# Cached sequences' values: fp32r products with both parts of the probabilities in one stationary, in two blocks of four page pairs

## What is computed

```python
ckv = concat([cache_ckv[pages].reshape(2048, 256), ckv_new])    # latent rows, also the values
kpe = concat([cache_kpe[pages].reshape(2048, 32), kpe_new])
k = rmsnorm(concat([einsum('lc,chd->lhd', ckv, w_uk), kpe]))    # 8 heads
s = einsum('qhd,khd->hqk', q, k) * SCALE                        # causal mask on the 8 new rows
p = softmax(s)
o_lat = einsum('hqk,kc->qhc', p, ckv)                           # the values, the product changed here
o = einsum('qhc,chd->qhd', o_lat, w_uv)
```

## Time and profile before

| what | us |
|---|---|
| median of three runs | 1565.51 (1563.53 to 1567.21) |
| span of the profiled execution | 1561.6 |
| PE busy in it | 1546.7 (99%) |
| DVE busy | 1042.6 (67%) |
| ACT busy | 631.2 (40%) |
| POOL busy | 581.8 (37%) |

### The profile page before, as it was taken

The page is one execution under the profiler, slowest core; times in us unless marked ns, Lnnn a source line. Parts: engine busy times, 40 slices in busy tenths (PEclk is TensorE's granted clock), DMA queues, the critical chain, the costliest instruction groups (busy, mean ns, idle before and its releaser), DMA issues.

```text
span 1561.6 us, 31760 instructions
## 1 busy us (share of the span) xinstructions
PE 1546.7 (99%) x11182; PEld 1475.9 (95%) x11182; DVE 1042.6 (67%) x1672; ACT 631.2 (40%) x1192; POOL 581.8 (37%) x604
## 2 busy tenths in 40 slices
PE   8999999999999999999999999999999999999998
PEld 8999999999999999588988888888999999999998
DVE  4998888512269975866777777774759988885011
ACT  6444445422221242464654445552434444354110
POOL 3165555445445654320000000013551655554342
PEclk9999999999999999999999999999999999999999
DMA  6133334223223332002122222212222333342222
GB/s 173 51 101 92 94 94 124 69 80 87 80 77 103 83 112 73 1 1 72 52 62 62 61 62 62 58 45 81 82 81 58 105 94 94 94 118 67 75 82 72
DMA packets 231405, 122.29 MB, mean 78 GB/s; under 512 B 28399, under 2 KB 228311, under 8 KB 231300
## 3 DMA queue, kind: packets, MB, share of 16 engines
q1 hardware_dynamic: 230238, 120.30, 27.4%
q10 hardware_dynamic: 1070, 0.74, 0.2%
HBM read 117.79 MB, written 3.58 MB: 78 GB/s over the span
## 4 chain that ended last, share of the span: by engine, by line
PE 93%; DVE 3%; issue 1%; ACT 1%; DMA 1%; SPq 0%; DVEq 0%; ACTq 0%
PE ps L474 40%; PE ps L1439 27%; PE ps L1790 12%; PE ps L1724 4%; PE ps L1710 2%; PE ps L1581 1%; PE ps L1635 1%; PE ps L1610 1%; PE ps L1753 1%; DMA x_nat<-in_x_sample 1%; PE ps L1625 1%; PE ps L1587 1%; PE ps L1592 0%; DVE xs L1999 0%; DVE xs_raw L1984 0%
## 5 line engine op out<-in xcount | busy, mean ns | idle before, releaser
L460 POOL TENSOR_TENSOR w_lobuf<-w_rawbuf,w_hibuf 128x256 fp32r<-128x256 f32 (+2 forms) x336 | 316.8, 974 | 355.1 <-ACT w_hibuf L453 355.1
L1439 PE MATMUL ps<-xs,w 128*128 128x288 f32 x3192 | 427.5, 296 | 2.2 <-DVE w L1913 2.2
L1439 PEld LDWEIGHTS ps<-xs,w 128*128 128x128 f32 x3192 | 426.8, 188 | 2.6 <-issue 2.6
L756 POOL TENSOR_TENSOR w<-w_raw,w 128x256 fp32r<-128x256 f32 x216 | 222.6, 1062 | 222.9 <-DVE w_raw L1901 139.2
L453 ACT ACTIVATE w_hibuf<-w_rawbuf 128x1024 fp32r<-128x1024 f32 (+1 forms) x90 | 104.8, 1164 | 359.6 <-PE ps L474 358.2
L474 PE MATMUL ps<-a_hi,w_hibuf 128*128 128x288 f32 x704 | 152.6, 297 | 0.0
L474 PE MATMUL ps<-a_hi,w_lobuf 128*128 128x288 f32 x704 | 152.1, 297 | 0.0
L474 PE MATMUL ps<-a_lo,w_hibuf 128*128 128x288 f32 x704 | 150.2, 294 | 0.0
L474 PE MATMUL ps<-x_hi,w_hibuf 128*128 128x288 f32 (+1 forms) x672 | 146.1, 299 | 1.6 <-DVE w_lobuf L2073 0.8
L474 PE MATMUL ps<-x_hi,w_lobuf 128*128 128x288 f32 (+1 forms) x672 | 144.5, 296 | 0.0
L474 PE MATMUL ps<-x_lo,w_hibuf 128*128 128x288 f32 (+1 forms) x672 | 144.4, 296 | 0.0
(11 more groups left out here) (320 smaller groups left out, 2722.7 us busy)
## 6 DMA issues: line engine op xcount, KB each, us to landing
w_raw<-in_ffn_w_gu SPq DMA_DIRECT2D x76, 256.0 KB, 2.9
up_rows<-in_ffn_w_gu SPq DMA_DIRECT2D x74, 256.0 KB, 3.1
c_nat<-in_cache_ckv SPq DMA_DIRECT2D x128, 128.0 KB, 2.0
w_rawbuf<-in_w_in SPq DMA_DIRECT2D x58, 256.0 KB, 3.1
w_rawbuf<-in_ffn_w_down SPq DMA_DIRECT2D x32, 384.0 KB, 4.0
w_rawbuf<-in_ffn_w_down SPq DMA_DIRECT2D x32, 320.0 KB, 3.4
w_rawbuf<-in_ffn_w_gu SPq DMA_DIRECT2D x24, 256.0 KB, 3.3
w_rawbuf<-in_w_out SPq DMA_DIRECT2D x16, 256.0 KB, 3.1
```

Source lines behind the costliest of these rows:

```text
L460: ins = pool.tensor_tensor(w_lobuf[:, r, part], w_rawbuf[:, r, part], w_hibuf[:, r % HIS, part].bitcast(F32), ALU.subtract)
L756: ins = pool.tensor_tensor(w7[b][:, slot, 1, part], w7_raw[b][:, slot, 1, part], w7[b][:, slot, 0, part].bitcast(F32), ALU.subtract)
L1439: mm = pe.matmul(ps[:, seven_bank(f, slot), 0:HALF], m, xs[:, slot, n, k, :], start=k == 0 and j == 0, stop=k == KH - 1 and j == 2)
```

## The change

For sequences r = 0 to 5, whose softmax is made within s = 1 to 6 (`stacked(s)`, s at most 6), the values become fp32r products. r = 6 (within s = 7) and r = 7 (after the loop) keep the f32 products.

- **Stationary**: `p_two`, for each page 128 columns: the high parts of the 64 probabilities and beside them the low parts. One matmul gives both results in 128 rows of the output. PE makes two such matmuls a page, with the high part `c_hi` and the low part `c_lo` of the page's latent rows as 256 moving columns: 32 in all, two for the new rows, and one in f32 for the denominator, whose sums DVE first completes by the new rows' and doubles to 128 columns.
- **PE's order**: four page pairs ahead of tile 10, four and the rest ahead of tile 14, the transposes of the result (now 128x128) inside tile 15.
- **ACT**: each exponential is made twice, first into `p_two` (high part) and then into `s_buf`; `p_done` rises after each half.
- **POOL**: for each pair a high part (product with a column of ones, 128x512) and a low part (128x512), sixteen in all; for each half of the probabilities a low part (128x512, and 64x64 for the new rows). Its order in sequence s: pairs 0 to 3, both halves of the probabilities, pairs 4 to 7, and then the squares of the rotary keys. `c_hi` has four buffers, so the high part of pair 4 waits until PE has used that of pair 0.
- **DVE**: its scaling moves to pair 7, its copying to the end of pair 7; the copying adds the rows of the low probabilities to those of the high ones (four instructions for two).
- **SP**: waits for two pairs used ahead of four pages; the two chunks of merge weights are loaded after the pages of sequence 7, when r = 5 is done, and ACT takes the high part of the first after pair 1 of sequence 7.

Cut to its core (the placing of the buffers is left out):

```diff
+        STACKED = NS - 2
+        PAIRS, EARLY_PAIRS = NP // 2, len(c_hi)
+        SPLITS = 2 * PAIRS + 2
+        def pair_made(r, j):
+            return r * SPLITS + (2 * EARLY_PAIRS + 1 if j < EARLY_PAIRS else 2 * j + 4)
 # SP
-            for t in range(2):
-                load_merge(t)
...
-                        sp.wait_ge(pages_used, used + (g + 1))
+                        sp.wait_ge(pages_used, used + 2 * (g + 1))
...
+            sp.wait_ge(lat_mm, STACKED)
+            for t in range(2):
+                load_merge(t)
             sp.wait_ge(page_mm, NS * NP)
 # POOL
+            def split_pair(r, b, j):
+                two = slice(2 * j, 2 * j + 2)
+                made = 2 * j + (1 if j < EARLY_PAIRS else 3)
+                pool.wait_ge(ct_tr, r * PAIRS + (j + 1))
+                pool.wait_ge(pages_used, r * PAIRS + (j + 1))
+                pool.tensor_tensor(c_hi[j % EARLY_PAIRS][:, :, :], c_nat[:, b, two, :], ones[:, 0:1, None].broadcast_to([P, 2, KL]), ALU.mult).then_inc(split_made, 1)
+                pool.wait_ge(split_made, r * SPLITS + made)
+                pool.tensor_tensor(c_lo[:, b, two, :], c_nat[:, b, two, :], c_hi[j % EARLY_PAIRS][:, :, :].bitcast(F32), ALU.subtract)\
+                    .then_inc(split_made, 1)
+            def probabilities_low(r, b, half):
+                t = slice(half * NP // 2, (half + 1) * NP // 2)
+                pool.wait_ge(p_done, r * 2 + (half + 1))
+                ins = pool.tensor_tensor(p_two[:, t, 1, :], s_buf[:, b, t, :], p_two[:, t, 0, :].bitcast(F32), ALU.subtract)
+                if half:
+                    ins = pool.tensor_tensor(p_two[0:TS, NP, 1, :], s_buf[0:TS, b, NP, :], p_two[0:TS, NP, 0, :].bitcast(F32), ALU.subtract)
+                ins.then_inc(split_made, 1)
             def squares(s, b, uses, prev, nxt):
+                if prev and stacked(s):
+                    for j in range(EARLY_PAIRS):
+                        split_pair(s - 1, 1 - b, j)
+                    for half in range(2):
+                        probabilities_low(s - 1, 1 - b, half)
+                    for j in range(EARLY_PAIRS, PAIRS):
+                        split_pair(s - 1, 1 - b, j)
 # ACT, soft_act
-                act.activation(s_buf[:, b, 0:NP // 2, :], s_buf[:, b, 0:NP // 2, :], ACT.Exp, scale=SCALE)
-                yield
-                act.activation(s_buf[:, b, NP // 2:NP, :], s_buf[:, b, NP // 2:NP, :], ACT.Exp, scale=SCALE)
-                act.activation(s_buf[0:TS, b, NP, :], s_buf[0:TS, b, NP, :], ACT.Exp, scale=SCALE).then_inc(p_done, 1)
-                yield
+                for half in range(2):
+                    t = slice(half * NP // 2, (half + 1) * NP // 2)
+                    last = half == 1
+                    if stacked(r + 1):
+                        act.activation(p_two[:, t, 0, :], s_buf[:, b, t, :], ACT.Exp, scale=SCALE)
+                        if last:
+                            act.activation(p_two[0:TS, NP, 0, :], s_buf[0:TS, b, NP, :], ACT.Exp, scale=SCALE)
+                    ins = act.activation(s_buf[:, b, t, :], s_buf[:, b, t, :], ACT.Exp, scale=SCALE)
+                    if last:
+                        ins = act.activation(s_buf[0:TS, b, NP, :], s_buf[0:TS, b, NP, :], ACT.Exp, scale=SCALE)
+                    ins.then_inc(p_done, 1)
+                    yield
 # PE, soft_pe
-                pe.wait_ge(p_done, r + 1)
+                if stacked(r + 1):
+                    for j in range(PAIRS):
+                        pe.wait_ge(split_made, pair_made(r, j))
+                        for u in range(2):
+                            t = 2 * j + u
+                            pe.matmul(ps[:, 7, 0:KL], p_two[:, t].rearrange("p h n -> p (h n)"), c_hi[j % EARLY_PAIRS][:, u, :], start=t == 0, stop=False)
+                            mm = pe.matmul(ps[:, 7, 0:KL], p_two[:, t].rearrange("p h n -> p (h n)"), c_lo[:, b, t, :], start=False, stop=False)
+                        mm.then_inc(pages_used, 1)
+                        if j < PAIRS - 1:
+                            yield
+                    for part in (new_hi, new_lo):
+                        pe.matmul(ps[:, 7, 0:KL], p_two[:, NP].rearrange("p h n -> p (h n)"), part[:, :], start=False, stop=False)
+                    pe.wait_ge(p_summed, r + 1)
+                    pe.matmul(ps[:, 7, KL:KL + 1], den_sum[:, :, :].rearrange("p h n -> p (h n)"), ones[:, 0:1], start=False, stop=True).then_inc(lat_mm, 1)
+                    yield
...
 # PE, pe_seq
+                        if prev and stacked(s):
+                            for _ in range({10: 4, 14: 4}.get(t, 0)):
+                                next(soft)
...
-                            if prev and t in (7, 8) and k == 1:
+                            if prev and k == 1 and t in ((7, 8, 15) if stacked(s) else (7, 8)):
                                 next(soft)
 # DVE, soft_dve
+                own(dve.tensor_tensor(den_sum[0:TS, 0, :], den_sum[0:TS, 0, :], s_buf[0:TS, b, NP, :], ALU.add), 6)
+                dve.tensor_copy(den_sum[:, 1, :], den_sum[:, 0, :]).then_inc(p_summed, 1)
```

More of the change, by code:

```diff
@@ L193, in layer @@
         cT = place("cT", [P, KL // P, T], F32, S2 + 15104)
-        c_new = place("c_new", [TS, KL], F32, kvg_at)
+        c_new = place("c_new", [TS, KL], F32, hi_at + 4 * DK * P + 4 * KD * P)
         head_ss = place("head_ss", [P, 2, NT, H], F32, S2 + 22048)
@@ L232, in layer @@
         s_new = place("s_new", [TS, NS, H, DS_], F32, sumsq_at)
-        o_lat = place("o_lat", [HQ, KL], F32, A0 + 35552)
-        den_sum = place("den_sum", [P, HQ], F32, A0 + 36576)
-        inv_den = place("inv_den", [HQ, 1], F32, A0 + 36832)
+        o_lat = place("o_lat", [P, KL], F32, A0 + 35552)
+        den_sum = place("den_sum", [P, 2, HQ], F32, hi_at + 4 * DK * P + 4 * KD * P + 4 * KL)
+        inv_den = place("inv_den", [P, 1], F32, A0 + 36832)
+        p_two = place("p_two", [P, NP + 1, 2, HQ], F32R, ring_at)
+        c_hi = [place(f"c_hi{j}", [P, 2, KL], F32R, at) for j, at in enumerate((
+            ring_at + 4 * (NP + 1) * 2 * HQ, hi_at, hi_at + 8 * KL, tb_at + 4 * NS * NP))]
+        c_lo = place("c_lo", [P, 2, NP, KL], F32R, A0)
+        new_hi = place("new_hi", [P, KL], F32R, tb_at + 4 * NS * NP + 8 * KL)
+        new_lo = place("new_lo", [P, KL], F32R, hi_at + 16 * KL)
+        assert 4 * (NP + 1) * 2 * HQ + 8 * KL <= 8 * DK * P and 4 * KD * P + 4 * KL <= 4 * DK * P
+        assert 4 * KD * P + 4 * KL + 8 * HQ <= 4 * DK * P and tb_at + 4 * NS * NP + 12 * KL <= A0
         pages = place("pages", [1, NS * NP], I32, tb_at)
@@ L802, in _ @@
             pool.memset(head_ss[:, :, :, :], 1.0).then_inc(filled, 1)
-            for n in range(n_gate + KD + 2, n_merge + 1):
+            for n in range(n_gate + KD + 2, n_merge):
                 split_lo(pool, n, n % RAWS, KD * P)
@@ L841, in _ @@
             pool.wait_ge(filled, 5)
-            def squares(s, b, uses, prev, nxt):
+            for part in (p_two[TS:P, NP, :, :], new_hi[TS:P, :], new_lo[TS:P, :]):
+                pool.memset(part.bitcast(F32), 0.0).then_inc(filled, 1)
+            pool.wait_ge(filled, 8)
+            pool.tensor_copy(new_hi[0:TS, :], c_new[:, :]).then_inc(filled, 1)
+            pool.wait_ge(filled, 9)
+            pool.tensor_tensor(new_lo[0:TS, :], c_new[:, :], new_hi[0:TS, :].bitcast(F32), ALU.subtract).then_inc(filled, 1)
+            pool.wait_ge(filled, 10)
+            def split_pair(r, b, j):
[14 more added lines that the diff above has]
+                ins.then_inc(split_made, 1)
+            def squares(s, b, uses, prev, nxt):
+                if prev and stacked(s):
[5 more added lines that the diff above has]
+                        split_pair(s - 1, 1 - b, j)
+                if not nxt:
+                    split_lo(pool, n_merge, n_merge % RAWS, KD * P)
                 for g in range(NP // 4):
@@ L1721, in soft_pe @@
                 yield
-                pe.wait_ge(p_done, r + 1)
+                if stacked(r + 1):
[13 more added lines that the diff above has]
+                    yield
+                    pe.wait_ge(rows_in, 9 * 16)
+                    pe.wait_ge(lat_scaled, r + 1)
+                    for k in range(2):
+                        tr = pe.transpose(ps[:, 7, k * P:(k + 1) * P], o_lat[:, k * P:(k + 1) * P], ident[:, :])
+                    tr.then_inc(lat_tr, 1)
+                    yield
+                    return
+                pe.wait_ge(p_done, r * 2 + 2)
                 for t in range(NP):
                     mm = pe.matmul(ps[0:HQ, 7, 0:KL], s_buf[:, b, t, :], c_nat[:, b, t, :], start=t == 0, stop=False)
-                    if t % 4 == 3:
+                    if t % 2:
                         mm.then_inc(pages_used, 1)
@@ L1763, in pe_seq @@
                         transpose_pair(s + 1, 1 - b, uses + b, 0)
-                    if prev and pp in (6, 7):
+                    if prev and not stacked(s) and pp in (6, 7):
                         next(soft)
@@ L2555, in dve_seq @@
```

(4 more changed lines are left out.)

48 lines of the change are left out of this document (31 added, 17 removed).

## The result

The changed kernel takes 1576.09 us (1574.64 to 1577.65, 4 runs), the kernel before 1565.17 us (1563.53 to 1567.21, 4 runs): ratio 1.0068, 95% interval 1.0053 to 1.0082. It is slower by 10.9 us; the forecast was 1573 us and slower.

A forecast was written before the change was run, and what follows sets the result against it. PE, busy 99% of the span, was taken to bound the kernel. Each sequence: -3.6 + 3.0 + 1.7 = +1.1 us; six +6.6, plus 0.5 for sequence 7 and edges; 1565.5 + 7.5, rounded to 1573 us, range 1558 to 1588.

The forecast's parts named there:

- the first wait: Ahead of tile 10, PE stands for two exponentials and POOL's low part of the probabilities: 3.0 us a sequence (2.7 to 3.6).
- POOL's chain: POOL's work from the probabilities' low parts to pair 7, needed by PE's second block: ready at 913.0 in sequence 4.
- PE's own work: Values on PE: 34 matmuls at 0.12 us plus the denominator, 4.4 us for 8.04, saving 3.6 us a sequence.
- its own signs of being wrong: In the profile after: `p_two` ready at tile 10, POOL's low parts at 1.0 us, or a wait elsewhere, likeliest for pages.
- POOL's prices: On POOL: high parts 1.04 us, low parts 1.27, the small low part for the new rows about 0.4.
- The rival of POOL ahead of the second block: PE finds pair 7 ready ahead of tile 14, only the wait at tile 10 is left: faster, 1559 us; chance 0.18.
- second wait: Within the pairs ahead of tile 14, PE stands for POOL's pair 7: 1.7 us a sequence (0 to 4.4).
- The taps: Four DVE instructions beside POOL's pairs 4 to 7 slow POOL by 0.4 us each, 1.6 us a sequence.
- the exclusion rival: POOL and DVE exclude each other: each of four taps costs POOL 0.74 us, +8 us in all, 1581; chance 0.10.
- the clock fall only in a rival: PE's clock falls to 0.50 after a wait, one unhidden fall in each of six sequences: +10 us, 1583; chance 0.15.
- lead I called "as before": DVE's lead over PE in pairs 0 to 4 of a sequence stays unchanged; no cost was put on it.
- Sequence 7 and the edges: All outside the six sequences: 0.5 us, with merge weights arriving about when ACT wants them, 0 to 1 us, once.

The follow-up runs named there:

- ninth kernel: The eighth kernel with ten f32 matmuls that serve nothing, overwriting nothing, filling PE's wait ahead of the first block: 1560.36 us, ratio 0.9962.
- third kernel: The changed kernel with ten f32 matmuls that serve nothing ahead of the first block's wait, so PE is busy while it waits: 1579.01 us, ratio 1.0086.
- first kernel: The changed kernel with ACT taking the first two merge-weight chunks' high parts after pairs 4 and 5 of sequence 7, not 1 and 2: 1566.60 us, ratio 1.0014.
- fifth kernel: The first kernel with the second block ahead of tile 15 instead of 14: 1565.09 us, ratio 0.9994.
- eighth: The first kernel with the high parts of pairs 4 to 7 made by ACT instead of POOL: 1566.88 us, ratio 1.0007.
- seventh: The fifth kernel with the first half of the probabilities made in two parts of four pages on ACT and POOL: 1565.01 us, ratio 0.9995.
- tenth: The seventh kernel with ACT making the high parts of pairs 4 to 7 and the second block ahead of tile 14 again: 1558.11 us, ratio 0.9946.
- fourth: The changed kernel without the low parts of the probabilities (their columns zero), so the first block waits for ACT alone: 1563.39 us, ratio 0.9991.

## Why the prediction was right, and where it was not

The sign and the time (3.1 us off) hold, and of the mechanism the first wait, POOL's chain and PE's own work. Two terms of the sum were mis-sized, in opposite directions. Two of its own signs of being wrong came true: waits appeared elsewhere, for the merge weights and for DVE (not for pages), and the clock did not stay at 1.00. (The sum as written adds 7.5 where its terms give 7.1; it would read 1572.6.)

- *PE's own work.* Forecast 4.4 us in place of 8.04. In the ninth kernel, at full clock, the blocks take 860.24 to 862.25 and 870.55 to 872.91, together 4.37. Right.
- *First wait.* Forecast 3.0 (2.7 to 3.6). In the six sequences it is 2.63, 2.64, 2.63, 2.64, 2.72 and 2.07 (from start to start, less the last transpose's own 0.11), at the lower end and below. From the exponential's start to the block it took 2.55 (860.70 to 863.25 in s = 3), forecast 2.54; but the exponential started 0.1 behind PE's arrival and not 0.5: the subtraction was done earlier, and only ACT's table load held it.
- *POOL's prices.* High part 1.04 (median), low parts 1.28 and 1.29: right. The small one 0.31, against 0.4. The last pair was ready at 13.0 us behind the first block's start in s = 1 to 4, forecast 13.4, and at 12.7 and 11.8 in s = 5 and 6. The rival of POOL ahead of the second block is out for s = 1 to 4, and holds for s = 5 and 6, where there was no second wait.
- *The taps.* The four of a sequence cost POOL's chain 1.27 us in all, forecast 1.6; the exclusion rival wanted 3.0. But they do not cost 0.3 each: POOL lost 0.49, nothing, 0.45 and 0.33 us. By the Trainium skill, "SBUF — State Buffer", "SBUF: two separate sides", the one of the two that starts first has the ports for its whole instruction, and the other waits. This trace agrees, within 0.2 us: of POOL's parts and DVE's taps, the one that started second always ended its own length less 0.13 to 0.20 us behind the end of the first (lines in the last section). The prediction took 0.4 a tap from sums of four and read it as no exclusion; there, too, the tap that started inside a part of POOL's was held, 1.11 us instead of 0.75. The rival failed not because nothing is excluded, but because DVE was the one held about as often as POOL.
- *Second wait*, forecast 1.7, found in four sequences as gaps of 0.41 to 0.55, so 0.3 to 0.4 of waiting, and not at all in two: **the first mis-sized term.** POOL was 0.4 us earlier than forecast, and PE 1.0 later. I had let the clock fall only in a rival. It fell to 0.50 behind all six first waits; the first block took 2.8 to 3.5 instead of 2.0 us, and PE came to the second at 11.2 us behind the first one's start (s = 3) and not at 10.3. At full clock it comes at 9.7 (third kernel, s = 2), so the fall cost PE 1.6 us. The third kernel shows the term as I had it, gaps of 1.6 to 2.4 us in its first four sequences, once the clock is kept. The Trainium skill, "TensorE: Matmul & The Clock Gate", "Why this matters for your kernels", advises against idle gaps above about 3 us; all six here were shorter, and the clock fell all the same. The rival's sentence that such a fall is partly hidden was right, its +10 us was not: in s = 1 to 5 the kernel that keeps the clock is at most 0.1 us faster. In s = 6, without a second wait, it is 1.0 us faster from the mark to the end of the second block, so there 1.0 of the 1.6 us was not hidden. The six sequences cost 0.5 us each instead of 1.1.
- *DVE*, whose lead I called "as before", a term of nothing. Between the marks of s = 2 and s = 3 two of its small steps took 0.99 and 1.26 us beside the two parts of POOL's pair 3 for the next sequence (842.80 and 843.91 us), against 0.29 and 0.23 in all eight sequences before; PE then stood 0.5 us for `cT_lo`, and this distance is 1.1 us longer than before, its neighbours' 0.4 and 0.5. By the trace this is a third cost; no run takes it apart.

```profile
843.00 0.99 DVE L2543 TENSOR_TENSOR k_inv<-page_ss,kpe_ss 128x128 f32<-128x128 f32 x1
844.02 1.26 DVE L2544 TENSOR_SCALAR k_inv<-k_inv 128x128 f32<-128x128 f32 x1
...
848.13 0.53 PE L1882 MATMUL ps<-kq_hi,cT_hi 128*128 128x288 f32 x2 [0.48 <-DVE cT_lo L2499]
```

- *Sequence 7 and the edges*, 0.5 us, with the merge weights at "0 to 1 us, once": **the second.** They cost 9.0 to 9.5 us, shown by the first kernel. The prediction named the weights' arrival without a working, though the numbers were at hand: SP issues a page every 1.69 us, so the sixteen pages of sequence 7 take it 27 us. It issued them in one row from 990.6 to 1018.4; when the second block of r = 5 ended, at 1002.0, nine of them still stood ahead of the weights. SP came to the weights at 1019.5 and ACT had them at 1023.3; it wanted them behind pair 1, at 1015.0. PE still had work for part of those 8.3 us and stood for 6.8; the half clock behind it, 6.8 us long, is the rest of the cost.

So 2.8 us for the six sequences and 9.0 for the weights stood in for 6.6 and 0.5, and the total came out near by luck in good part.

## What to carry to other kernels

A saving on the engine that bounds a loop is worth what the next chain leaves of it: work out when the last product of the helping engine is ready, counted from the same event, before pricing the saving. When an issue is moved past others in one queue, follow it to its first consumer by clock time, and look at what stands behind that consumer on its engine: one chunk of weights 8 us late cost three times as much as the six sequences together. And when a helping engine gets work, look at what it slows on the engine that shares its ports, in the steps that the bounding engine waits for. A fall of PE's clock costs little where another chain is the bound; measure it by filling the wait, in a version that has no later wait to give the time back to.

## What the hardware showed that I had not expected

- The granted clock fell to 0.50 for 3.4 us behind every first wait of the changed kernel. In the fifth kernel, with the same waits, it fell behind three of six; in the eighth, with the same waits again, behind five; in the seventh and tenth, with waits of 1.7 us, and in the fourth, with 1.3 us, behind none of the six. Why the same wait is followed by a fall in one sequence and not in another stays open.
- POOL and DVE hold each other up, and the one that comes second pays. DVE's taps took 1.27 and 1.52 us where POOL's parts were on their way first (s = 3 of the changed kernel), against 0.75 in the earlier trace rows; on average 1048 ns against 780 in the same stretch before:

```profile
871.86 1.30 POOL L882 TENSOR_TENSOR c_lo<-c_nat,c_hi 128x512 fp32r<-128x512 f32 x1
...
872.43 1.27 DVE L2245 SCALAR_TENSOR_TENSOR y<-ext,cols,y 128x512 f32<-128x512 f32 x1
...
873.88 1.27 DVE L2245 SCALAR_TENSOR_TENSOR y<-ext,cols,y 128x512 f32<-128x512 f32 x1 [0.18 <-DVE y L2245]
...
875.33 1.52 DVE L2245 SCALAR_TENSOR_TENSOR y<-ext,cols,y 128x512 f32<-128x512 f32 x1 [0.18 <-DVE y L2245]
```

Read with POOL's lines of s = 3 in the section on the result: `c_lo` (871.86 to 873.16) loses nothing, and the tap that starts inside it ends at 873.70; `c_hi` starts inside this tap and ends at 874.60; the next tap starts inside `c_hi` and ends at 875.15, the next `c_lo` at 876.30, the last tap at 876.85. Each second one ends 0.54 to 0.55 us (tap), 0.90 (`c_hi`) or 1.15 (`c_lo`) behind the first, where alone they take 0.74, 1.04 and 1.28. I had priced this on POOL's side alone, and on DVE's side it reached the path in s = 2.
